# Deeper buffers and wider weight loads in the last attention pass of a hybrid decoder block, with due times shifted by stage

## What is computed

```
h = RMSNorm(x); proj = h @ w_in                       # 1024 x 10768
mixer A (delta rule, 8 heads x 128):
  q,k,v = silu(causal conv4(.)); q,k L2-normalised
  per chunk: T = inverse of a lower triangular matrix (by Newton steps here)
  u = T (beta v);  w = T (beta k exp(gc))
  v_new = u - w S;  o = (q exp(gc)) S + (q k^T decay) v_new
  S = S exp(g_last) + (k decay)^T v_new               # serial from chunk to chunk
  o = RMSNorm(o) * silu(z)
mixer B (attention, 3 groups x 4 heads x 128):
  partial rotary; (window, dilation) = (128,1), (512,4), (2048,16)
  group results of a head joined by their softmax denominators
x = x + (sigmoid(ga) (oA @ w_proj_a) + sigmoid(gb) (oB @ w_proj_b)) @ w_out
x = x + (silu(h2 @ w_gate) * (h2 @ w_up)) @ w_down    # h2 = RMSNorm(x), width 2816
out = RMSNorm(x)
```

## Time and profile before

| | |
|---|---|
| median of the runs | 3322.48 us |
| the profiled execution | 3319.85 us |
| its span on the slowest core (core 2) | 3318.3 us |
| spans of the 8 cores | 3285.1 to 3318.3 us |
| TensorE busy | 3123.9 us, 94% of the span |
| VectorE, ScalarE, GpSimd busy | 54%, 48%, 28% |
| mean granted clock of TensorE, core 2 | 0.983 |

### The profile page before, as it was taken

The page is one execution under the profiler, slowest core; times in us unless marked ns, Lnnn a source line. Parts: engine busy times, 40 slices in busy tenths (PEclk is TensorE's granted clock), DMA queues, the critical chain, the costliest instruction groups (busy, mean ns, idle before and its releaser), DMA issues.

```text
span 3318.3 us, 62314 instructions; the slowest of 8 cores (3285.1 to 3318.3 us)
## 1 busy us (share of the span) xinstructions
PE 3123.9 (94%) x24278; PEld 1989.7 (60%) x24678; DVE 1778.1 (54%) x4012; ACT 1580.1 (48%) x4149; POOL 916.0 (28%) x1253
## 2 busy tenths in 40 slices
PE   5899999999999999999868999999899999999999
PEld 3587777777777777777656544444344444444444
DVE  4777767768677686676735565665221222222222
ACT  4767767666777767667634434333211211111111
POOL 4444544445444444443320112111111000000000
PEclk9999999999999999999978999999999999999999
DMA  7533553256225353523386343343576245345422
GB/s 165 121 76 68 82 91 67 65 78 95 69 67 88 65 90 73 80 63 71 62 146 124 101 141 125 112 147 105 104 115 105 89 77 102 89 64 114 89 39 89
DMA packets 406744, 307.93 MB, mean 93 GB/s; under 512 B 237744, under 2 KB 369456, under 8 KB 406448
## 3 DMA queue, kind: packets, MB, share of 16 engines
q1 hardware_dynamic: 284400, 224.54, 25.9%
q0 software_dynamic: 122048, 79.37, 18.1%
HBM read 276.23 MB, written 67.70 MB: 104 GB/s over the span
## 4 chain that ended last, share of the span: by engine, by line
PE 82%; DMA 7%; DVE 6%; ACT 2%; POOL 1%; issue 1%; SPq 0%; DVEq 0%; POOLq 0%
PE psf L401 79%; DVE arena L429 3%; PE psf L404 2%; DMA ob_d<-arena 2%; DVE arena L438 2%; DMA arena<-w_in 1%; ACT arena L412 1%; POOL arena L429 1%; ACT arena L407 1%; DMA arena<-w_gate_up 1%; DMA arena<-arena 0%; DVE arena L433 0%; DMA arena<-w_down 0%; DMA arena<-gcT_d 0%; DMA arena<-c_cs 0%
## 5 line engine op out<-in xcount | busy, mean ns | idle before, releaser
L401 PE MATMUL psf<-arena 128*128 128x128 bf16 (+3 forms) x21715 | 3034.1, 296 | 118.3 <-ACT arena L412 18.4
L401 PEld LDWEIGHTS psf<-arena 128*128 128x128 bf16 x22050 | 1849.6, 103 | 1193.1 <-ACT arena L412 34.2
L429 POOL TENSOR_TENSOR arena<-arena 128x4 f32<-128x4 f32 (+4 forms) x704 | 642.1, 924 | 962.9 <-DVE arena L429 418.1
L429 DVE TENSOR_TENSOR arena<-psf,arena 128x128 f32<-128x128 f32 (+3 forms) x944 | 471.6, 523 | 745.6 <-PE psf L401 726.1
L407 ACT ACTIVATE arena<-psf 128x512 f32<-128x512 f32 (+2 forms) x770 | 428.6, 566 | 768.6 <-PE psf L401 731.0
L412 ACT CAST arena<-psf 128x512 bf16<-128x512 f32 (+1 forms) x896 | 470.7, 544 | 269.1 <-PE psf L401 261.2
L438 DVE SCALAR_TENSOR_TENSOR arena<-arena,psf 128x512 bf16<-128x512 f32 (+2 forms) x640 | 342.0, 546 | 209.3 <-PE psf L401 166.1
L407 ACT ACTIVATE arena<-arena 128x128 bf16<-128x128 f32 (+6 forms) x592 | 271.9, 477 | 356.0 <-DVE arena L429 311.4
L429 DVE TENSOR_TENSOR arena<-arena,psf 128x512 bf16<-128x512 bf16 (+1 forms) x640 | 328.5, 523 | 180.5 <-PE psf L401 157.0
L412 ACT COPY arena<-psf 128x256 f32<-128x256 f32 (+2 forms) x467 | 224.3, 485 | 211.7 <-PE psf L404 144.7
L404 PE MATMUL psf<-ident_b,arena 128*128 128x128 bf16 x1918 | 196.1, 226 | 68.5 <-DVE arena L438 27.2
(11 more groups left out here) (34 smaller groups left out, 555.6 us busy)
## 6 DMA issues: line engine op xcount, KB each, us to landing
arena<-w_gate_up POOLq DMA_DIRECT2D x40, 1024.0 KB, 11.5
arena<-x SPq DMA_DIRECT2D x64, 512.0 KB, 4.1
ob_d<-arena SPq DMA_DIRECT2D x192, 130.0 KB, 2.1
arena<-ob_d SPq DMA_DIRECT2D x32, 780.0 KB, 4.4
arena<-gcT_d SPq DMA_DIRECT2D x64, 256.0 KB, 3.6
x_d<-arena SPq DMA_DIRECT2D x32, 512.0 KB, 2.8
arena<-x_d SPq DMA_DIRECT2D x32, 512.0 KB, 3.5
out<-arena SPq DMA_DIRECT2D x32, 512.0 KB, 2.6
```

The costliest lines, as they stand in the source:

```text
L401: P.emit("pe", lambda e: e.matmul(out, lhsT=lhsT, rhs=rhs, start=start, stop=stop), reads=reads, excl=excl, cost=c)
L429: P.emit(eng, lambda e: e.tensor_tensor(out=out, in0=in0, in1=in1, op=op), reads=reads, writes=writes, excl=excl, cost=c)
```

## The change

Three things change. In the last pass, the staging tiles go from 2 to 9 and the `c_cs` tiles from 2 to 10, of which the 8 new ones are used; the new tiles lie where the streams had their data, and `P.seed` makes them wait for every user of that data. The rotary sum goes from GpSimd to VectorE there. The loads of ga, gb, pa and pb go from 16 loads of 256 columns to 8 of 512. And each instruction of the streams gets a bias on its due time: -10 in stage B, 0 in stage A2, +25 in stage A1 (except in the first two units' prologue).

```diff
@@ schedule
-                i.prio = -(t0 + (t1 - t0) * n_ / len(li))
+                i.prio = -(t0 + (t1 - t0) * n_ / len(li) + i.bias)
@@ stream: merge and its use (emit sets ins.bias = self.bias)
                 for gg in list(act_):
+                    P.bias = gg[1]
                     try:
-                        next(gg)
-                        yield
+                        next(gg[0])
                     except StopIteration:
                         act_.remove(gg)
+                        continue
+                    finally:
+                        P.bias = 0.0
+                    yield
...
-            xs_ = [stageB(units[ui][0], units[ui][1], ui)]
+            xs_ = [(stageB(units[ui][0], units[ui][1], ui), -10.0)]
             if ui + 1 < NU:
-                xs_.append(stageA2(units[ui + 1][0], units[ui + 1][1], ui + 1))
+                xs_.append((stageA2(units[ui + 1][0], units[ui + 1][1], ui + 1), 0.0))
             if ui + 2 < NU:
-                xs_.append(stageA1(units[ui + 2][0], units[ui + 2][1], ui + 2))
+                xs_.append((stageA1(units[ui + 2][0], units[ui + 2][1], ui + 2), 25.0))
@@ phase2b
+    SG, CS = list(stg), list(cs)
+
+    def deepen():
+        AX = A.part(k.off_r + 12288, 2560)
+        more = P.keys("s0_", "s1_", "ngc", "egc", "edl", "qbeta", "egl", "cw", "dnw", "mhalf", "two_i")
+        nk_ = []
+        for i in range(7):
+            SG.append(AX.alloc(128, (2, 130), F32))
+            nk_ += ["t_stg%d%s" % (i + 2, e_) for e_ in ("", "m", "o", "d0", "d1")]
+        for i in range(8):
+            CS.append(AX.alloc(128, (64,), F32))
+            nk_.append("t_cs%d" % (i + 2))
+        P.seed(nk_, more)
+
+    def stage(J):
+        i = J % 2 if J < 5 * NT else J % 9
+        return SG[i], "t_stg%d" % i
@@ proj
-        c_ = cs[J % 2]
-        ck = "tn_cs%d" % (J % 2)
+        ci = J % 2 if J < 5 * NT else 2 + J % 8
+        c_ = CS[ci]
+        ck = "tn_cs%d" % ci if ci < 2 else "t_cs%d" % ci
...
-        TT(P, "pool", tm[:, :, 0:32], t1, t2, ALU.add, ...)
+        TT(P, "pool" if J < 5 * NT else "dve", tm[:, :, 0:32], t1, t2, ALU.add, ...)
@@ attn and attn_v
-        st, sk = stg[J % 2], "t_stg%d" % (J % 2)
+        st, sk = stage(J)
@@ the loop over J
         if J == 5 * NT:
+            deepen()
             phase3w(k)
@@ phase3w
-    for q in range(4):
+    for q in range(2):
         for nm, wt_, src, nk in ws:
-            wload(k, wt_[:, :, q * 256:(q + 1) * 256], src, (OFF[nm] if nm in OFF else 0) + q * 256, 256, nk, "w%s%d" % (nm, q))
+            c0 = (OFF[nm] if nm in OFF else 0) + q * 512
+            DMA(P, "pool", wt_[:, :, q * 512:(q + 1) * 512], src[0:nk * 128, c0:c0 + 512].rearrange("(kc p) c -> p kc c", p=128),
+                writes=["w%s%d" % (nm, 2 * q), "w%s%d" % (nm, 2 * q + 1)])
```

More of the change, by code:

```diff
@@ L25 @@
     __slots__ = ("eng", "fn", "deps", "odeps", "dma", "need", "sem", "val", "cost", "seg", "idx",
-                 "prio", "nrem", "succ", "fin", "waits")
+                 "prio", "bias", "nrem", "succ", "fin", "waits")
     def __init__(self, eng, fn, dma):
@@ L910, in stream @@
         yield from stageA1(units[0][0], units[0][1], 0)
[L911 removed]
+        yield from merge((stageA1(units[1][0], units[1][1], 1), 0.0), (stageA2(units[0][0], units[0][1], 0), 0.0))
         for ui in range(NU):
[L913 removed]
+            xs_ = [(stageB(units[ui][0], units[ui][1], ui), -10.0)]
             if ui + 1 < NU:
[L915 removed]
+                xs_.append((stageA2(units[ui + 1][0], units[ui + 1][1], ui + 1), 0.0))
             if ui + 2 < NU:
[L917 removed]
+                xs_.append((stageA1(units[ui + 2][0], units[ui + 2][1], ui + 2), 25.0))
             yield from merge(*xs_)
```

5 lines of the change are left out of this document (3 added, 2 removed).

## The result

The changed kernel takes 0.9886 [0.984, 0.9932] of the time of the kernel before (nine runs of each). On 3322.5 us that is 38 us less, 23 to 53 by the interval. The profiled execution took 3278.14 us, and its slowest core is core 4 with 3276.5 us. The forecast of 3284 us is met by the ratio, but two of its terms were wrong and largely cancelled each other.

The account below looks back on a forecast made before the run. TensorE, busy 94% of the span, was taken as the bound, with gains only where it idles or runs slow. Last pass 35.3 plus 3 us for 1640 to 1700 gave 38 off 3322.5: 3284 us, range 3245 to 3325.

Parts of the forecast that it names:

- Last pass, -35.3 us: Last pass: deeper buffers remove store and table waits, 45.4 us, less 4, 2.5 and 3.6 us, gaining 35.3 us.
- joins, I count 4 us: Last pass: join reads of 780 KB keep two buffers; one traced wait of 3.7 us, counted as 4 us remaining.
- Wide loads, 0: Weight loads: 17 us less of load, priced at nothing because nobody waits for these weights before about 1840 us.
- The sum on VectorE, 0: Last pass: 32 sums add 10 to 15 us of VectorE work beside TensorE; priced at nothing unless joins pile up.
- Late first tables and the smaller cover, 2.5 and 3.6 us: Last pass: 2.5 us idle (0 to 8) waiting for first new tiles; 32 projection matmuls done later cost 3.6 us.
- 1640 to 1700, +3 us: Between mixers and last pass: stage A2 chains spread over more matmuls, 3 us gained, between -5 and +8.
- Mixers, 0: Mixers, 200 to 1640: shifted due times change nothing; median distance falls from 28 to 18 matmuls, still above one round trip.
- The bound of 38 us on the mixers' gain: Mixers: only waits for computing engines can move, 38 us in all, so at most 38 us gained.
- the load moves to the joins: Rival, last pass: wide weight packets slow tables to 18 us and join reads to about 17; costs about 20 us; chance 0.20.
- The mixers gain too: Rival, mixers: grouped A2 steps take half of the 38 us of waits, 3265 us, or all, 3246; chance 0.24.
- Urgent steps stall TensorE: Rival, mixers: stage B's 256 steps wait for VectorE; if two thirds do, 78 us lost, 3362 us; chance 0.10.
- signs named for being right: Last pass: ob_d store waits gone, clock near 1.00 from about 1700, pass 115 to 125 us instead of 165.

Follow-up runs that it names:

- e11: Changed kernel with last-pass joins ten tiles later and planner costs of 20 for join reads, 16 for the first sixteen new tiles' stores: ratio 0.9843 to before.
- e6: Changed kernel with its weight loads 256 columns wide again: ratio 0.987 to the kernel before.
- e3: Kernel before with only the deeper last-pass buffers; due times, GpSimd's sum and 256-column loads as before: ratio 0.9945.
- e10: Changed kernel with the last pass's rotary sum back on GpSimd, wide loads kept: ratio 0.9853 to the kernel before.
- e2: Changed kernel with all due-time shifts at 0, so the last-pass edits alone: ratio 0.9908 to the kernel before.
- e7: Changed kernel with stage A1's shift of +25 alone, stage B at 0: no ratio; profiled execution 3260.75 us, core span 3245.0 us.
- e12: Changed kernel with joins ten tiles later, measured DMA durations as planner costs, and stage B's shift at 0: ratio 0.9755 to the kernel before.
- e4: Changed kernel with the four joins of the last pass placed ten tiles later: ratio 0.9844 to the kernel before.
- e9: Changed kernel with joins ten tiles later and their reads also depending on a later tile's store: ratio 0.9864 to the kernel before.

## Why the prediction was right, and where it was not

- **Last pass, -35.3 us: 26.5.** The mechanism was right: the waits for `ob_d` stores in the pass fell from 39.4 to 3.8 us (mean over cores, 1620 to 1870) and those for tables from 10.6 to 4.6, one wait at the start, as written. The term that failed is "joins, I count 4 us". It took 12.8 us of VectorE, and once it is gone (e11) the pass gains 39.8 us. I read the 3.7 us of the earlier trace rows as the price of a join; it was the rest after other waits had let the read catch up. With those waits gone VectorE came to the join sooner, and the read no sooner.
- **Wide loads, 0:** about 6 us of pass lost beside a sum on VectorE (e6; not clear of the scatter in time), a gain beside a sum on GpSimd (e3 against e10). "Nobody waits behind them" was wrong on both sides: the joins do, and with the sum on GpSimd VectorE does.
- **The sum on VectorE, 0:** right next to wide loads (e10), about 15 us next to narrow ones (e3 against e6, less the 1.7 us by which e2's pass is longer than the changed kernel's). Eleven of the 24 us for which the sum was held on core 3 are the two pauses for semaphores. It was a cover of the sort that should have been named: the row to look at was GpSimd's queue with its weight loads, behind which the first sum stands.
- **Late first tables and the smaller cover, 2.5 and 3.6 us.** VectorE waits once for the first table, 4 to 5 us on every core of the changed kernel, and TensorE has no wait behind it: the forty matmuls that cover it (here on core 4) took 8.6 us, 1672.86 to 1681.48, and not the 4.5 of the earlier trace rows, since the first 16 needed 1.89 us for each eight and four gaps of 0.46 us stood between the eights for ScalarE's copy (L414). So the cover held, but was itself longer than counted. The 3.6 us are not separated further.
- **1640 to 1700, +3 us: nothing.** Its idle time is 12.7 us in place of 12.8. The wait for the stores of tiles under 160 remained, as written.
- **Mixers, 0: 19.8 us gained.** This is the step that failed most, and it failed twice. I gave as the gain's cause that the four matmuls of an A2 step stand together. The piece of the order shown above does that, but over the whole mixers a run of A2 matmuls is 2.95 long in the mean before and 2.90 after. And I took a distance of 18 matmuls in the median as safe, where the short round trips are a few per cent of all and a median doesn't show them.
- **The bound of 38 us on the mixers' gain was not a safe one.** It was the sum of visible waits. Stage A1's shift alone gives 39.5 us by streams' end and 33.7 by core span, nearly the whole bound, while TensorE's idle time between 200 and 1600 fell by only 13.4 us (40.5 to 27.1, e2 to e7, mean of cores 1, 3, 5 and 7). Core 3 shows it against before. Its row in e12, columns as in the earlier trace rows:

```profile
200.00:1600.00 1400.00, 1373.65 (x14697) 1087.90 (x14696) 1028.34 (x2464) 982.31 (x2856) 644.22 (x892) 1.00 0.40 77
```

These are 330 matmuls more than before in the same 1400 us. By their columns they are 24 us of work at full clock, less than the 32 us that their number says, as few of them are 512 wide. The idle time fell by 13.4 us (39.7 to 26.3), so some 10 of the 24 us came out of the busy time. A likely reason is the overlap of the records: forty matmuls of 256 columns complete in 4.53 us, 0.113 us each, but one record of that form lasts 0.274 us in the mean on this core, so a wait of up to 0.16 us can lie under the record ahead. No run separates these short waits.

The rivals: *the load moves to the joins* happened in place and kind, 9.6 us more on VectorE in the mean and a wait of 16.2 on core 4, against 20 counted. Its table landing, 18 us by the packets' sizes, is 15.4 measured; its join read, 17, is 10.7, and what made the wait long was the store ahead of the read, which I had left out. The Trainium skill (DMA: Bandwidth & Descriptors, Queues, rings and completion order) says that an engine takes turns between its queues a whole packet at a time; a packet there is a bundle of descriptors, and that it takes longer with wider ones was my own step. e6 agrees with that step, with tables of 15.4 against 10.3 us. *The mixers gain too* happened in size, 20 us, by another cause. *Urgent steps stall TensorE* is true of stage B's shift: it costs 14 us (15 to 21 by core spans) of the 60 to 80 named, and stage A1's shift hides it. The forecast of 3284 us was met since 9 us too much (and 3 for 1640 to 1700) and 20 us too little stood beside each other, and since the slowest core gained less than the mean one (41.8 against 47.3 us of span); that the number fits so closely is luck. Two of the signs named for being right did not come: the clock was to be near 1.00 from 1700 on and is 0.93 in 1700 to 1800, and the last pass was to lose 40 to 50 us (115 to 125 in place of 165) and lost 26.5.

## What to carry to other kernels

When a wait goes away, ask for the next instruction with an external input on the same queue, and work out its own chain in full: here a store's landing plus a read's, 26 us under load (1690.44 to 1716.67 on core 4), though the trace showed 3.7 us for it. A planner that orders by "what can start first" must be told the durations of DMAs under the load in which they run; moving the calls in the source by ten tiles moved the first join by two places on VectorE's queue. When a queue pauses between issues, look at the program's own semaphores first. Visible idle time understates what better spacing of dependent chains can give, here by nearly half: count the completed matmuls and their columns in a fixed window, and the round trips that are too short, not their median.

## What the runs showed of the hardware

- Wide loads make their neighbours slower at the same share of the engines: 1008-byte packets of 115 ns against 504-byte ones of 70 ns, with queue 0 at 73.6 and 73.5%; a 32 KB table 15.4 against 10.3 us, a 130 KB store 14.0 against 10.6, a 780 KB read 10.7 against 9.7.
- A weight load costs GpSimd 0.8 to 1 us to issue, and an operation of 0.5 us behind seventeen of them started 24 us late, 11 of these for semaphores that the kernel shares.
- Of 24 us more work that core 3 did in the same 1400 us (e12 against before), 13.4 us came out of TensorE's idle time and some 10 out of its busy time.
- The same first 200 us, with TensorE's order equal up to there, hold 1465 to 1598 matmuls in different executions (the changed kernel, e4, e6, e9, e10, e11; means of four cores), 13 us at the mixers' pace; comparisons of streams' end by a single profile are no better than that.
